# A two-layer trunk on one core: x in two column halves, squares of the first norm on other engines, last rows turned unscaled

## The reference

```python
def rms_norm(x, g):
    xf = x.astype(jnp.float32)
    y = xf * lax.rsqrt(jnp.mean(xf * xf, axis=-1, keepdims=True) + NORM_EPS)
    return (y * g.astype(jnp.float32)).astype(x.dtype)
...
h = x
for layer in range(DEPTH):
    ...
    h = h + fox_conformer_mixer(rms_norm(h, norm_mix0[i]), w_in0[i], ...)
    ...
    h = h + swiglu_ffn(rms_norm(h, norm_ffn[layer]), w_gate[layer], w_up[layer], w_down[layer])
return rms_norm(h, final_norm)
```

## Time and profile before

| | us |
|---|---|
| median of 3 runs | 2926.29 |
| lowest, highest | 2925.61, 2928.42 |
| the profiled execution, its own time | 2924.83 |
| its span | 2923.3 |
| TensorE busy in it | 2781.6 (95%) |
| VectorE, ScalarE, GpSimd busy | 1894.0, 1401.8, 545.3 |
| granted TensorE clock, mean | 0.974 |

### The profile page before, as it was taken

The page is one execution under the profiler, slowest core; times in us unless marked ns, Lnnn a source line. Parts: engine busy times, 40 slices in busy tenths (PEclk is TensorE's granted clock), DMA queues, the critical chain, the costliest instruction groups (busy, mean ns, idle before and its releaser), DMA issues. The chain is left out here.

```text
span 2923.3 us, 43721 instructions
## 1 busy us (share of the span) xinstructions
PE 2781.6 (95%) x15925; PEld 2435.1 (83%) x15925; DVE 1894.0 (65%) x2476; ACT 1401.8 (48%) x2136; POOL 545.3 (19%) x509
## 2 busy tenths in 40 slices
PE   5999999999999999999998889989899999999997
PEld 5888788888888888877877778778788888888886
DVE  4799675555555547678677686684575565555555
ACT  3477554444444444464463563654354444444443
POOL 4001141111210216010010110120241011111214
PEclk8999999999999999999999999999999999999998
DMA  5554355555555555455454543553555555555553
GB/s 178 159 173 145 128 188 187 187 188 187 191 191 191 186 179 190 165 171 160 131 183 137 171 144 123 187 180 114 186 185 184 191 187 187 189 190 189 193 170 105
DMA packets 246088, 502.25 MB, mean 172 GB/s; under 512 B 10920, under 2 KB 11529, under 8 KB 244393
## 3 DMA queue, kind: packets, MB, share of 16 engines
q1 hardware_dynamic: 237232, 473.99, 49.3%
q0 software_dynamic: 5888, 25.79, 2.7%
q10 hardware_dynamic: 2808, 0.38, 0.1%
HBM read 491.64 MB, written 8.49 MB: 171 GB/s over the span
## 5 line engine op out<-in xcount | busy, mean ns | idle before, releaser
L957 DVE TENSOR_TENSOR w_lo<-raw,w_hi 128x1024 fp32r<-128x1024 f32 (+1 forms) x912 | 1151.1, 1297 | 728.8 <-ACT w_hi L563 727.3
L563 ACT ACTIVATE w_hi<-raw 128x1024 fp32r<-128x1024 f32 (+1 forms) x912 | 905.9, 1036 | 973.5 <-PE acc L1796 957.4
L1803 PE MATMUL acc<-xs,w_hi 128*128 128x512 f32 x5120 | 1298.6, 401 | 33.2 <-ACT w_hi L563 22.2
L1803 PEld LDWEIGHTS acc<-xs,w_hi 128*128 128x128 f32 x5120 | 945.1, 192 | 216.8 <-issue 22.8
L1796 PEld LDWEIGHTS acc<-xs,w_lo 128*128 128x128 f32 x5120 | 670.1, 192 | 44.7 <-DVE w_lo L957 13.5
L1796 PE MATMUL acc<-xs,w_lo 128*128 128x256 f32 x5120 | 690.9, 285 | 10.1 <-DVE w_lo L957 10.1
L1803 PE MATMUL acc<-hs,w_hi 128*128 128x512 f32 x1920 | 469.1, 393 | 14.1 <-issue 10.2
L1803 PEld LDWEIGHTS acc<-hs,w_hi 128*128 128x128 f32 x1920 | 352.3, 190 | 82.1 <-issue 10.6
L570 ACT ACTIVATE tmp<-acc 128x256 f32<-128x256 f32 x448 | 170.0, 383 | 300.0 <-PE acc L1796 261.8
L1796 PEld LDWEIGHTS acc<-hs,w_lo 128*128 128x128 f32 x1920 | 251.4, 191 | 12.6
L1796 PE MATMUL acc<-hs,w_lo 128*128 128x256 f32 x1920 | 255.3, 282 | 0.0
(11 more groups left out here) (288 smaller groups left out, 1655.3 us busy)
## 6 DMA issues: line engine op xcount, KB each, us to landing
raw<-in_w_in SPq DMA_DIRECT2D x136, 1024.0 KB, 5.2
raw<-in_w_gate SPq DMA_DIRECT2D x88, 1024.0 KB, 5.2
raw<-in_w_up SPq DMA_DIRECT2D x88, 1024.0 KB, 5.2
raw<-in_w_down SPq DMA_DIRECT2D x64, 1024.0 KB, 5.1
raw<-in_w_out SPq DMA_DIRECT2D x48, 1024.0 KB, 5.1
raw<-in_w_down SPq DMA_DIRECT2D x32, 768.0 KB, 4.6
L<-g_rows POOLq DMA_DIRECT2D x4, 1536.0 KB, 7.8
I<-g_rows POOLq DMA_DIRECT2D x4, 1536.0 KB, 11.8
```

The costliest lines, as they stand in the source:

```text
L563: nc.scalar.activation(w_hi[:, c % 2, k], raw[:, c, k], ACT.Copy).then_inc(hi_ready, 2 if kc == 1 else 1)
L957: nc.vector.tensor_tensor(w_lo[:, c % 2, k], raw[:, c, k], w_hi[:, c % 2, k].bitcast(F32), ALU.subtract).then_inc(lo_ready, 2 if kc == 1 e ...
L1803: mm(acc[:, m, :], w_hi[:, c % 2, k, cols], r[:, kk], start=kk == 0, stop=end, skip_group_check=True)
```

## The change

At the start, x comes in two transfers of 1024 columns each (x_half, x_in). TensorE turns the first eight rows on the first, the constants in the middle, then the other eight; ScalarE copies in that order. VectorE waits for four rows of xT at a time. SyncE starts the weights on x_half. ScalarE makes w_hi of chunk 0 between the second and the third xs step. GpSimd's squares are gone: in the first group ScalarE squares xT in two instructions of 128x2048 into sq_all, and VectorE sums them in a tree of four. The norm of that group is made after chunk 2 (NORM_AT).

At the end, ScalarE scales twelve rows by the gain alone (xg) during the last group's chunks 1 to 3, VectorE the last four. TensorE turns them into eight banks (four aux, four acc) without waiting for the norm. The sum of squares is made per frame in a column: for each half of the frames five matmuls with one column, over sq_acc and the four squared last rows (gt). The factor rstd_c is the scale of the copies out of the banks, four of 128x512 on ScalarE for the first 128 frames and four on VectorE for the second.

```diff
-            sp_e.dma_start(stage[:], x.rearrange("o (t p) d -> p (o t) d", p=P)).then_inc(x_in, 16)
+            for half, landed in enumerate((x_half, x_in)):
+                cols = slice(half * D // 2, (half + 1) * D // 2)
+                sp_e.dma_start(stage[:, :, cols], x[0, :, cols].rearrange("(t p) d -> p t d", p=P)).then_inc(landed, 16)
...
-            sp_e.wait_ge(const_in, 16 * 15)
+            sp_e.wait_ge(x_half, 16)
             walk(sp_e, load, peel_first=False)
             for t in range(TT):
-                sp_e.wait_ge(y_out, 15 + t)
+                sp_e.wait_ge(y_out[t], 4)
...
-            link(pool.memset(sq_acc[:], 0.0))
-            for k in range(KT):
-                pool.wait_ge(x_copied, k + 1)
...
-                nc.gpsimd.tensor_tensor(sq_one[:], xT[:, k], xT[:, k], ALU.mult).then_inc(sq_made, 1)
-                pool.wait_ge(sq_made, k + 1)
-                nc.gpsimd.tensor_tensor(sq_acc[:], sq_acc[:], sq_one[:], ALU.add).then_inc(sq_added, 1)
...
+            for k in range(0, 8, 2):
+                x_copy(k)
             act.wait_ge(const_pe, 6)
...
+            for k in range(8, KT, 2):
+                x_copy(k)
...
-            split_hi(0, 0, 4, 0)
-            split_hi(0, 0, 4, 1)
+                if c == 1:
+                    split_hi(0, 0, 4, 0)
+                    split_hi(0, 0, 4, 1)
...
+                    if s.name == "glu" and here.starts and c == 0:
+                        for half in range(2):
+                            nc.scalar.activation(sq_all[:, half * 2048:(half + 1) * 2048],
+                                                 xT[:, 8 * half:8 * half + 8].rearrange("p k t -> p (k t)"), ACT.Square)\
+                                .then_inc(sq_tiles, 1)
+                    if s is segs[-1] and isinstance(i, int) and i == s.n - 1 and c:
+                        act.wait_ge(resid_added, 4 * (s.resid + c))
+                        for k in range(4 * c - 4, 4 * c):
+                            last = nc.scalar.activation(xg[:, k], xT[:, k], ACT.Copy, scale=vec[:, G_FINAL + k:G_FINAL + k + 1])
+                        last.then_inc(xg_made, 1)
...
-            dve.wait_ge(x_copied, KT)
             for c in range(4):
+                dve.wait_ge(x_copied, 4 * c + 4)
...
+                        for n in (2048, 1024, 512):
+                            dve.wait_ge(sq_tree, (2048, 1024, 512).index(n))
+                            nc.vector.tensor_tensor(sq_all[:, 0:n], sq_all[:, 0:n], sq_all[:, n:2 * n], ALU.add)\
+                                .then_inc(sq_tree, 1)
...
+            nc.vector.tensor_tensor(gt[:], last_rows, last_rows, ALU.mult).then_inc(y_sq, 1)
...
+                last = nc.vector.tensor_scalar(xg[:, k], xT[:, k], vec[:, G_FINAL + k:G_FINAL + k + 1], None, ALU.mult)
...
+            for g in range(4):
+                dve.wait_ge(y_pe, 2 * g + 2)
+                nc.vector.tensor_scalar(stage[:, 1, g * GW:(g + 1) * GW], y_bank(g, 1), rstd_c[:, 1:2], None, ALU.mult)\
+                    .then_inc(y_out[1], 1)
...
-                    if s.name in NORMED and here.starts and c == 1:
+                    if s.name in NORMED and here.starts and c == NORM_AT(s):
                         norm(g.norm)
...
+            for g in range(3):
+                pe.wait_ge(xg_made, g + 1)
+                if g == 2:
+                    pe.wait_ge(acc_free, 4 * n_groups)
+                y_turn(g)
+            pe.wait_ge(sq_added, 16 * 4 + 12)
+            pe.wait_ge(y_sq, 1)
+            for t in range(TT):
+                fr = slice(t * P, (t + 1) * P)
+                mm(acc[:, 3, t:t + 1], sq_acc[:, fr], ones[:, 0:1], start=True, stop=False)
+                for m in range(GM):
+                    last = mm(acc[:, 3, t:t + 1], gt[:, m, fr], ones[:, 0:1], start=False, stop=m == GM - 1)
```

More of the change, by code:

```diff
@@ L235, in trunk @@
         stage = sb("stage", [P, TT, D], at=h1)
+        sq_all = sb("sq_all", [P, KT * T], at=h1)
+        xg = sb("xg", [P, KT, T], at=h1 + 16384)
         vrow = sb("vrow", [P, 5, P], at=h_at)
@@ L389, in tiles, with y_bank, NORM_AT @@
             return t[:, 2 * a:2 * a + 2].rearrange("p b t c -> p (b t) c")
+        def y_bank(g, t):
+            return aux[2 * g + t][:] if g < 2 else acc[:, 2 * g - 4 + t, :]
+        def NORM_AT(s):
+            return 2 if s.name == "glu" else 1
         def tick(steps, n=1):
@@ L622, in scalar_program, with x_copy @@
                            .rearrange("(k p) n -> p k n", p=P)).then_inc(wsm_in[0], 16)
+            def x_copy(k):
+                act.wait_ge(x_trans, k // 2 + 1)
+                for h in range(2):
+                    nc.scalar.activation(xT[:, k + h], acc[:, (k // 2) % 4, h * T:(h + 1) * T], ACT.Copy)\
+                        .then_inc(x_copied, 1)
+            for k in range(0, 8, 2):
+                x_copy(k)
             act.wait_ge(const_pe, 6)
@@ L678, in visit @@
                         post(before)
-                    if here.starts and c == 1 and g.norm is not None and g.kind != "resid" and s.name in NORMED:
+                    if s.name == "glu" and here.starts and c == 0:
[8 more added lines that the diff above has]
+                        last.then_inc(xg_made, 1)
+                    if here.starts and c == NORM_AT(s) and g.norm is not None and g.kind != "resid" and s.name in NORMED:
                         norm_act(act, g.norm)
@@ L1154, in vector_program @@
             R, i = resid_no(here), here.i
-            dve.wait_ge(sq_added, 16 * 4 + 4 * i)
             for m in range(GM):
@@ L1687, in tensor_program, with x_turn @@
             mm, tr = nc.tensor.matmul, nc.tensor.transpose
+            def x_turn(k):
+                if k >= 8:
+                    pe.wait_ge(x_copied, k - 6)
+                for h in range(2):
+                    for t in range(TT):
+                        last = tr(acc[:, (k // 2) % 4, h * T + t * P:h * T + (t + 1) * P],
+                                  stage[:, t, (k + h) * P:(k + h + 1) * P], ident[:])
+                last.then_inc(x_trans, 1)
+            pe.wait_ge(const_step, N_CONST_PE)
+            pe.wait_ge(x_half, 16)
+            for k in range(0, 8, 2):
+                x_turn(k)
             pe.wait_ge(const_in, 16 * 15)
-            pe.wait_ge(const_step, N_CONST_PE)
             tr(aux[0][:, 0:NVEC], vrow[0:NVEC, 0, :], ident[0:NVEC, 0:NVEC]).then_inc(const_pe, 1)
@@ L1699, in tensor_program @@
             pe.wait_ge(x_in, 16)
-            for k in range(0, KT, 2):
-                if k >= 8:
-                    pe.wait_ge(x_copied, k - 6)
-                for h in range(2):
-                    for t in range(TT):
-                        last = tr(acc[:, (k // 2) % 4, h * T + t * P:h * T + (t + 1) * P],
-                                  stage[:, t, (k + h) * P:(k + h + 1) * P], ident[:])
-                last.then_inc(x_trans, 1)
+            for k in range(8, KT, 2):
+                x_turn(k)
             def norm(n):
```

73 lines of the change are left out of this document (34 added, 39 removed).

## The result

The changed kernel took 2904.3 us in the median of six runs (2889.14 to 2907.83), against 2925.95 (2924.06 to 2929.78) for the kernel before on the same chip: a ratio of 0.991, 95% interval 0.9883 to 0.9937. The same kernel measured twice more gave medians of 2903.1 and 2901.14 us and ratios of 0.9925 and 0.9921, 2904.3 and 2903.2 on the same base. So the first measurement fell on the fast side of the kernel's scatter, and the miss of the range hangs on that; but the forecast of 2907.4 was too high against all three.

A forecast was written before the change was run, and what follows sets the result against it. TensorE was taken as the bound, busy 2781.6 of 2923.3 us (95%), with time to gain only where it waits. Start 14.2 - 3 - 1.5 = 9.7 plus end 9.2 makes 18.9 us: 2907.4 from 2926.29, range 2901 to 2915.5.

The forecast's parts named there:

- The start undelayed: First group, constants landing as before: chunk 3 starts at 42.1 instead of 56.33, a gain of 14.2 us.
- the third rival: First group: squares and tree put chunk 2's w_hi and w_lo behind TensorE's need; start's gain gone, 2917.1 us, chance 0.05.
- The constants later by 3 us: Start: weights sent right behind x hold up the constants on the other queue, 3 us off the start's gain.
- The first rival: Start: constants held back by the weights, a delay of 6 to 10 us; time 2914.4 us, chance 0.18.
- The clock at the turns: Start: TensorE at 1.2 GHz when turning the constants and x's second half, 1.5 us off the start's gain.
- The end: Behind the last weight matmul: second output transfer issued at 2907.7 instead of 2916.9, a gain of 9.2 us.
- The sum: Both ends together: 9.7 us at the start and 9.2 at the end, a gain of 18.9 us.
- the second rival: Start: no delay of the constants and no lost clock; gain 23.4 us, time 2902.9 us, chance 0.13.
- The middle, taken as unchanged: Between the two ends: the change touches only the ends, so no gain or loss was counted here.
- The rival on the slower side: After the earlier, gappier start TensorE stays at 1.2 GHz; with eight further chunks so, 2952 us; chance 0.03.

The follow-up runs named there:

- e12: The changed kernel measured again with nothing altered, in another measurement: 2901.14 us, ratio 0.9921 to the kernel before.
- e5: The changed kernel measured again with nothing altered, in another measurement: 2903.1 us, ratio 0.9925 to the kernel before.
- e7: The changed kernel without SyncE's wait for half of x, so the first four weight chunks are issued right behind x: 2898.61 us in one run.
- e9: The changed kernel with the unscaled turns of the first three row groups placed behind the sums of squares on TensorE: 2902.89 us, ratio 0.9918.

## Why the prediction was off, step by step

- **The start undelayed, 14.2 us: right; it measured 13.85.** Steps foreseen for TensorE at 21.2, 28.2, 30.1, 35.7 and 42.1 came at 22.02, 28.55, 30.55, 36.11 and 42.48. The slack of w_hi and w_lo in chunk 2 held, and the third rival (waits inside the group) did not come: the one wait, 0.45 us for w_lo of chunk 0, had been foreseen with 0.8.
- **The constants later by 3 us: this step failed.** They came 0.45 us later in the first profile, and -0.04 and 0.33 in e12 and e5. The row I took it from, 69 packets against 49, has x in full flow; I let the weights fill their queue from 7.14 on. They fill it from 11, when the constants are mostly through. The first rival, a delay of 10 with the time 2914.4, needs the weights in the queue from the start: e7 shows 6.7 us then. That is also more than 3, so the rate of one for one, 612 rows in 3.1 us, was wrong as well: the queues do move one for one (162 to 162), but at the last only 32 to 36 of the 162 are constants. The Trainium skill (DMA: Bandwidth & Descriptors, Queues, rings and completion order) has an engine drain a whole packet of 9 to 17 descriptors from a queue row before it turns to the next. The delay that I estimated by it, 6 to 10 us, fits e7 and not this change; the profile's packets, 187 to 186, show no queue favoured over the other. The other half of that argument, 124-row constants on few engines, fits e7's 32 to 36.
- **The clock at the turns, 1.5 us: this step failed too.** TensorE was at 1.2 GHz at the constants' turns and most of x's, as I said it would be. But the 14.2 us above are read from rows in which it was so already: the constants' turns are 0.21 us apart in both kernels and take the same 1.94 us up to ScalarE's first copy (11.92 to 13.86, 12.37 to 14.31). I took that price off a second time. The first weight matmul is 0.82 us late (22.02 against 21.2); 0.45 of that is the constants', the other 0.4 the x turns at half speed, and the wait for w_lo, shorter than foreseen, takes that in. The reason I gave, the idle time from 9.4 to 15, did not come either: the turns ran to 10.9, at half speed from their first on. What the clock is worth there shows e12, at 2.4 GHz from 10.70: chunk 3 starts 1.86 us earlier, 0.49 of it from earlier constants. So 1.5 was about its size, but as a gain over 14.2, in some executions, and not as a loss.
- **The end, 9.2 us: right, 9.9.** The sums are 2.4 us, not 3.0: I priced them at 0.15 each by the norm's six, two of which are 256 columns wide; the sums' are one column wide, 0.12 each. The root starts 6.0 us behind the last weight matmul, not 7. The clock stayed up, as assumed, and e9 shows a case where it did not: its sums took 4.4 us. The scaled copies xg lay under other work, as said.
- **The sum.** 4.5 us were taken off the start, and 0.35 are seen. By the rows after, 13.85 + 9.9 = 23.75 and 2926.29 - 23.75 = 2902.5. That is the number of the second rival, "no delay and no lost clock", 2902.9, to which I gave 0.13, and the runs agree: 2904.3, 2903.1, 2901.1. Its mechanism is only half what happened: there was next to no delay, but the clock was low; that this cost nothing beyond the 14.2 is luck of that sum. For it I had named one ground, the smaller packets, which no run tested; a better one, that a transfer does not fill its queue at once, could be had from the DMA view of before: x, issued at 1.05, moved 14 packets in the microsecond from 2 and 38 to 53 in each of the next three.
- **The middle, taken as unchanged: right in the mean, but no part of the range.** One kernel's executions lie within 22 us; three runs of before within 2.8 us did not show that. The range had 1.9 us below the likeliest full gain, less than the median of six such runs moves. That the first measurement fell below the range and the other two would not have is this scatter.
- The rival on the slower side, a clock that stays low after the earlier start, had nothing for it: the clock rose inside the first sixteen matmuls.

## What to carry to other kernels

How long a large stream delays small transfers depends on what is left of them when its packets reach the engines, here from 2 us behind its issue on: the stream was held until the load ahead of it was half in, and the small ones passed first. Put independent TensorE work into the wait ahead of a short chain of small matmuls: it leaves the chain, and it keeps the clock at 2.4 GHz for it (here 2.95 us of turns, 5.1 us of time, in one profile). Before a step is charged with a slow clock, look whether the rows that it is summed from have it already; and where a view prints a full clock, compare the spacing of like instructions. When a few runs lie close together, don't take that for the scatter of one kernel, and don't set a trace's whole difference down to the edit: split it at the borders of the edit first (here 13.85, 11.1 and 9.9) and measure the same kernel again.

## What was not expected of the hardware

- The same kernel's middle took 2828.2 and 2843.7 us in two executions, with 96 and 113 us at 1.2 GHz and waits for X of 2.9 and 8.7 us. Over fourteen profiles, idle time and half of the busy time at 1.2 GHz explain the middle to within 1.6 us.
- TensorE's first turns ran at half speed, 0.21 us apart instead of 0.11, up to 10.7 us in one execution of a kernel and 16.4 in another; the granted clock's records begin only there.
